# Retention in a two-block kernel: V projected token-major, value matmuls moved behind the next head's first unit, gate units reordered

## The reference

```python
def second_block(x, ...):
    h = rmsnorm(x, g_mix)
    proj = h @ w_in
    xc, gb, gc, q, k, v, g_sw, gate_a, gate_r = split(proj, ...)
    y_a = (gb * conv(gc * xc)) @ w_a_out
    qf = rotary(q by heads) * 256 ** -0.5        # 4 heads, 256 wide
    kf = rotary(k by heads)
    vf = v by heads                              # 4 heads, 512 wide
    ret = retention forward + strict retention backward (qf, kf, vf)
    # = ((q k^T) * decay(n - m)) v for each head, over all 512 x 512 pairs
    ret = (ret - mean) * rsqrt(var + EPS) * g_ret        # over the 512 of a head
    y_r = (ret * silu(g_sw)) @ w_r_out
    merged = sigmoid(gate_a) * y_a + sigmoid(gate_r) * y_r
    x = x + merged @ w_o
    x = x + ffn(rmsnorm(x))
    return rmsnorm(x)
```

## Time and profile before

| | |
|---|---|
| median of 3 runs | 1593.28 us (1589.33 to 1594.75) |
| span of the profiled execution, first to last instruction | 1585.1 us |
| TensorE busy in the span | 1515.8 us, 96% |
| VectorE, ScalarE, GpSimd busy | 704.2, 589.0, 92.0 us |
| mean granted clock of TensorE | 0.973 of full |
| the four heads of the retention stage | 665.38 to 923.09 us, 257.71 us |

### The profile page before, as it was taken

One profiled execution on the slowest core, in us unless ns is written; L12 is line 12 of the kernel. 1 busy time (PEld: TensorE's weight loads), 2 busy tenths in 40 slices (PEclk: granted clock), 3 DMA queues, 4 the chain that ended last, 5 costly groups with the idle time before them and its releaser, 6 DMA issues.

```text
span 1585.1 us, 20029 instructions
## 1 busy us (share of the span) xinstructions
PE 1515.8 (96%) x7068; PEld 1247.0 (79%) x7068; DVE 704.2 (44%) x1078; ACT 589.0 (37%) x955; POOL 92.0 (6%) x97
## 2 busy tenths in 40 slices
PE   7799998998989999999999999999998999999997
PEld 4578886887768888887787878887876888888886
DVE  4443256764465442344453524454445333333332
ACT  5232335653433334333333344443333333332321
POOL 5100500000000000000000023210000000000000
PEclk9799899998989999999999999999998999999999
DMA  9963320000333333331121213325232333333321
GB/s 328 328 135 95 106 60 9 1 2 14 89 134 89 100 97 102 93 94 53 53 80 52 79 54 93 93 80 157 82 96 63 106 93 93 105 92 99 99 84 53
DMA packets 243191, 147.87 MB, mean 93 GB/s; under 512 B 21490, under 2 KB 237758, under 8 KB 241732
## 3 DMA queue, kind: packets, MB, share of 16 engines
q1 hardware_dynamic: 239652, 131.63, 28.5%
q0 software_dynamic: 3488, 15.58, 2.9%
HBM read 138.81 MB, written 7.34 MB: 92 GB/s over the span
## 4 chain that ended last, share of the span: by engine, by line
PE 67%; issue 25%; DMA 3%; DVE 2%; ACT 2%; POOL 0%; DVEq 0%; POOLq 0%; SPq 0%; ACTq 0%
PE ps L368 50%; PE ps L1449 3%; PE ps L1731 3%; PE ps L1627 3%; PE ps L1641 2%; DMA w_raw<-in_w_in_dram 2%; PE ps L1708 1%; PE ps L1471 1%; PE ps L1526 1%; DMA bias_line<-bias_lines 1%; PE ps L1519 1%; DVE ret_val L1386 0%; PE ps L1615 0%; DMA rel_bias_sb<-in_rel_bias_dram 0%; PE ps L1494 0%
## 5 line engine op out<-in xcount | busy, mean ns | idle before, releaser
L385 DVE TENSOR_TENSOR w_lo<-w_raw,w_hi 128x1024 fp32r<-128x1024 f32 (+1 forms) x221 | 268.2, 1218 | 324.5 <-ACT w_hi L380 320.7
L380 ACT ACTIVATE w_hi<-w_raw 128x1024 fp32r<-128x1024 f32 (+1 forms) x221 | 228.9, 1043 | 32.4 <-DMA w_raw<-in_w_in_dram 18.8
L368 PE MATMUL ps<-g_hi,w_hi 128*128 128x512 f32 x704 | 181.0, 399 | 1.9 <-ACT g_hi L789 1.6
L368 PE MATMUL ps<-g_hi,w_lo 128*128 128x512 f32 x704 | 175.6, 392 | 0.0
L368 PE MATMUL ps<-g_lo,w_hi 128*128 128x512 f32 x704 | 174.1, 390 | 0.0
L368 PEld LDWEIGHTS ps<-g_hi,w_hi 128*128 128x128 f32 x704 | 131.8, 189 | 33.5 <-issue 4.9
L368 PEld LDWEIGHTS ps<-g_hi,w_lo 128*128 128x128 f32 x704 | 133.3, 189 | 28.1
L368 PEld LDWEIGHTS ps<-g_lo,w_hi 128*128 128x128 f32 x704 | 132.5, 188 | 27.6
L392 ACT ACTIVATE temps<-ps 128x512 f32<-128x512 f32 x68 | 40.7, 598 | 262.2 <-PE ps L368 262.2
L368 PE MATMUL ps<-f_hi,w_hi 128*128 128x512 f32 x352 | 90.3, 398 | 1.6 <-ACT f_hi L789 1.6
L368 PE MATMUL ps<-f_hi,w_lo 128*128 128x512 f32 x352 | 88.6, 395 | 0.0
(11 more groups left out here) (329 smaller groups left out, 2141.7 us busy)
## 6 DMA issues: line engine op xcount, KB each, us to landing
w_raw<-in_w_in_dram SPq DMA_DIRECT2D x95, 512.0 KB, 3.9
w_raw<-in_w_ff_gate_dram SPq DMA_DIRECT2D x22, 512.0 KB, 3.8
w_raw<-in_w_ff_up_dram SPq DMA_DIRECT2D x22, 512.0 KB, 3.7
w_raw<-in_w_in_dram SPq DMA_DIRECT2D x36, 256.0 KB, 4.3
w_ada_shift_scale<-in_w_ada_dram SPq DMA_DIRECT2D x8, 1024.0 KB, 20.2
w_raw<-in_w_r_out_dram SPq DMA_DIRECT2D x16, 512.0 KB, 4.3
w_raw<-in_w_ff_down_dram SPq DMA_DIRECT2D x16, 512.0 KB, 4.2
w_ada_gate<-in_w_ada_dram SPq DMA_DIRECT2D x2, 2048.0 KB, 12.9
```

The lines of the kernel that those rows point to most:

```text
L368: mm = pe.matmul(bank, w[:, slot, k], mov[:, k0 + k], start=first and n == 0 and k == 0, stop=last and n == 2 and k == kts - 1)
L380: act.activation(whi[:, slot, 0:kts], raw[:, slot, 0:kts], ACT.Copy).then_inc(hi_done, 1)
L385: nc.vector.tensor_tensor(wlo[:, slot, 0:kts], raw[:, slot, 0:kts], whi[:, slot, 0:kts].bitcast(F32), ALU.subtract).then_inc(lo_done, 1)
```

## The change

- V is projected token-major. Each of the four v units of a head now holds two of the eight 128-row blocks of the head's 1024 x 512 weights (`load_rows`: rows of 512 floats in place of 128), and the unit runs 4 x 6 matmuls with a block of the activations stationary and the 512 weight columns moving (`v_unit`). The four units add up in PSUM banks 4 to 7, one bank for each block of 128 tokens. The transposes and `v_t` are gone; `v_hi` and `v_lo` are made from the banks after the last v unit.
- The scores go before the fourth v unit, into banks 0 to 3. The p products are made at step 6 of the head, the v split at step 7.
- The value matmuls of a head (`read_out`) run after the first q unit of the next head; those of the last head after the first gate unit.
- POOL starts on a head's sum when that head's `ret` is there, no longer after all 16 tiles.
- The gate units of a head come as four silu, then two sigmoid.
- The two loops over heads are written out on every engine; `strip2` and the raw q have other places.

```diff
-PHASE_OUTS = (16, 8, 1, KT, 3 * KT, 2 * KT, 8 * RET_HEADS, 16 + KT, KT, KT, 2 * FT, KT)
+PHASE_OUTS = (16, 8, 1, KT, 3 * KT, 2 * KT, 4 * RET_HEADS, 16 + KT, KT, KT, 2 * FT, KT)
...
-RS_BANK = [4, 5, (O_QKV + 4) % 4, (O_QKV + 5) % 4]
-PV_BANK = [5, 6, 7, 4]
+RS_BANK = [(O_QKV + j) % 4 for j in range(4)]
...
-        strip2 = sb("strip2", [P, STRIP], R + 87)
-        v_t = sb("v_t", [P, 2, S], R + 91)
+        strip2 = sb("strip2", [P, STRIP], R + 107)
+        q_raw = sb("q_raw", [P, 2, S], R + 91)
...
-        qk_raw = sb("qk_raw", [P, 4, S], R + 131)
+        k_raw = sb("k_raw", [P, 2, S], R + 131)
...
+        def half_rows(t, u):
+            return t[:, u % SLOTS].rearrange("p k n -> p (k n)").rearrange("p (a n) -> p a n", a=2)
...
+            def load_rows(u, src):
+                sp.wait_ge(hi_done, u - 3)
+                sp.wait_ge(lo_done, u - 3)
+                sp.dma_start(half_rows(raw, u), src).then_inc(raw_in[u % SLOTS], 16)
...
-            with sp.Fori(0, 4) as it:
-                for k in range(8):
-                    if k < 4:
-                        cut = it * 256 + (3072 + 1024 * (k // 2) + (k % 2) * P)
-                    else:
-                        cut = it * 512 + (5120 + (k - 4) * P)
-                    load(it, 8, U_QKV + k, w_in2_v[:, :, wide(cut)])
...
+            for h in range(RET_HEADS):
+                for k in range(4):
+                    cut = h * 256 + 3072 + 1024 * (k // 2) + (k % 2) * P
+                    load(None, 0, U_QKV + 8 * h + k, w_in2_v[:, :, cut:cut + P])
+                for c2 in range(4):
+                    load_rows(U_QKV + 8 * h + 4 + c2, w_in2_v[:, 2 * c2:2 * c2 + 2, 5120 + 512 * h:5632 + 512 * h])
+            for h in range(RET_HEADS):
+                for n in range(6):
+                    cut = 7168 + h * 512 + n * P if n < 4 else GR_COL + h * 256 + (n - 4) * P
+                    load(None, 0, U_GATE + 6 * h + n, w_in2_v[:, :, cut:cut + P])
...
-            pool.wait_ge(m["ret_ev"], 16)
...
+            for h in range(RET_HEADS):
+                pool.wait_ge(m["ret_ev"], 4 * h + 4)
+                if h:
+                    pool.wait_ge(m["mu_mm"], h)
...
+            def ret_out(h):
+                for t in range(4):
+                    act.wait_ge(m["rpv_mm"], 4 * h + t + 1)
+                    a.activation(ret[:, 4 * h + t], ps[:, 4 + t], ACT.Copy).then_inc(m["ret_ev"], 1)
...
+            for h in range(RET_HEADS):
                 for k in range(8):
-                    act_convert(act, it, 8, U_QKV + k + AHEAD)
-                    dst = qk_raw[:, k] if k < 4 else v_t[:, k % 2]
-                    act_out(act, it, 8, U_QKV + k, dst, O_QKV + k, ACT.Copy)
+                    u = U_QKV + 8 * h + k
+                    act_convert(act, None, 0, u + AHEAD)
+                    if k == 0 and h == 0:
+                        act.wait_ge(lo_done, u + AHEAD + 1)
+                    if k < 4:
+                        act_out(act, None, 0, u, (q_raw if k < 2 else k_raw)[:, k % 2], O_QKV + 4 * h + k, ACT.Copy)
+                    if k == 0 and h:
+                        ret_out(h - 1)
...
-                    if k >= 5:
-                        v_round(k - 5)
-                for j in range(3):
-                    p_round(j)
-                v_round(3)
-                p_round(3)
-                for t in range(4):
-                    count = at(it, 4, t + 1)
-                    apart(act, it)
-                    act.wait_ge(m["rpv_mm"], count)
-                    a.activation(tile_of(ret, it, 4, t), ps[:, PV_BANK[t]], ACT.Copy).then_inc(m["ret_ev"], 1)
...
+                    if k == 6:
+                        for j in range(4):
+                            act.wait_ge(m["pm_done"], 4 * h + j + 1)
+                            a.activation(p_hi[:, j], p_f[:, j % 2], ACT.Copy).then_inc(m["ph_done"], 1)
+                    if k == 7:
+                        act.wait_ge(unit_done, u + 1)
+                        for j in range(NI):
+                            a.activation(v_hi[:, j], ps[:, 4 + j], ACT.Copy).then_inc(m["vh_done"], 1)
...
+            for h in range(RET_HEADS):
+                for n in range(6):
+                    u, o = U_GATE + 6 * h + n, O_GATE + 6 * h + n
+                    act_convert(act, None, 0, u + AHEAD)
+                    if n < 4:
+                        act_out(act, None, 0, u, sg[:, n], o, ACT.Silu)
                     else:
-                        act_out(act, it, 12, U_GATE + k, tile_of(sig_r, it, 4, 2 * hh + n), O_GATE + k, ACT.Sigmoid)
+                        act_out(act, None, 0, u, sig_r[:, 2 * h + n - 4], o, ACT.Sigmoid)
+                    if n == 0 and h == 0:
+                        ret_out(RET_HEADS - 1)
...
-                def v_rest(t):
-                    dve.wait_ge(m["vh_done"], at(it, 4, t + 1))
-                    cut = slice(t * P, (t + 1) * P)
-                    v.tensor_tensor(v_lo[:, :, cut], ps[:, 4 + t].rearrange("p (j e) -> p j e", j=NI),
-                                    v_hi[:, :, cut].bitcast(F32), ALU.subtract).then_inc(m["vl_done"], 1)
...
-                    if k in (5, 6):
-                        v_rest(k - 5)
-                dve.wait_ge(m["decay_done"], at(it, 1, 1))
-                p_mult(0)
-                p_mult(1)
-                p_rest(0)
-                v_rest(2)
-                p_mult(2)
-                p_rest(1)
-                v_rest(3)
-                p_mult(3)
-                p_rest(2)
-                p_rest(3)
-                own.end(RET_HEADS)
...
+                    if k == 6:
+                        dve.wait_ge(m["decay_done"], h + 1)
+                        p_mult(0)
+                        p_mult(1)
+                        p_rest(0)
+                        p_mult(2)
+                        p_rest(1)
+                        p_mult(3)
+                        p_rest(2)
+                        p_rest(3)
+                    if k == 7:
+                        for j in range(NI):
+                            dve.wait_ge(m["vh_done"], 4 * h + j + 1)
+                            v.tensor_tensor(v_lo[:, j], ps[:, 4 + j], v_hi[:, j].bitcast(F32),
+                                            ALU.subtract).then_inc(m["vl_done"], 1)
...
-            with pe.Fori(0, RET_HEADS) as it:
-                def v_trans(t):
-                    pe.wait_ge(evac, at(it, 8, O_QKV + 5 + t))
-                    for j in range(NI):
-                        mm = trans(ps[:, 4 + t, blk(j)], v_t[:, t % 2, blk(j)])
-                    mm.then_inc(m["vtr_mm"], 1)
-                def scores(j):
+            def v_unit(h, c2):
+                u = U_QKV + 8 * h + 4 + c2
+                pe.wait_ge(hi_done, u + 1)
+                pe.wait_ge(lo_done, u + 1)
+                if h and c2 == 0:
+                    pe.wait_ge(m["ret_ev"], 4 * h)
+                for j in range(NI):
+                    for n, (x, w) in enumerate(((g_hi, whi), (g_hi, wlo), (g_lo, whi))):
+                        for kk in range(2):
+                            mm = pe.matmul(ps[:, 4 + j], x[:, 2 * c2 + kk, blk(j)], half_rows(w, u)[:, kk],
+                                           start=c2 == 0 and n == 0 and kk == 0, stop=c2 == 3 and n == 2 and kk == 1)
+                mm.then_inc(unit_done, 1)
+            def scores(h):
+                pe.wait_ge(m["qkl_done"], 4 * h + 4)
+                for j in range(4):
                     for n, (k, q) in enumerate(((k_hi, q_hi), (k_lo, q_hi), (k_hi, q_lo))):
                         for t in range(2):
                             mm = pe.matmul(ps[:, RS_BANK[j]], k[:, t, blk(j)], q[:, t], start=n == 0 and t == 0,
                                            stop=n == 2 and t == 1)
                     mm.then_inc(m["rs_mm"], 1)
-                for k in range(8):
-                    pe_unit(pe, it, 8, U_QKV + k, 8, O_QKV + k, g_hi, g_lo)
-                    if k >= 5:
-                        v_trans(k - 5)
-                pe.wait_ge(m["qkl_done"], at(it, 4, 4))
-                for j in range(4):
-                    if j < 2:
-                        pe.wait_ge(m["vl_done"], at(it, 4, j + 1))
-                    scores(j)
-                v_trans(3)
-                pe.wait_ge(m["pm_done"], at(it, 4, 2))
+            def read_out(h):
                 for t in range(4):
-                    if t in (1, 2):
-                        pe.wait_ge(m["vl_done"], at(it, 4, t + 2))
                     for n, (w, p) in enumerate(((v_hi, p_hi), (v_lo, p_hi), (v_hi, p_lo))):
                         for j in range(NI):
-                            if t == 0 and n != 1:
-                                pe.wait_ge(m["ph_done" if n == 0 else "pl_done"], at(it, 4, j + 1))
-                            mm = pe.matmul(ps[:, PV_BANK[t]], w[:, j, blk(t)], p[:, j], start=n == 0 and j == 0,
+                            if t == 0:
+                                pe.wait_ge(m[("ph_done", "vl_done", "pl_done")[n]], 4 * h + j + 1)
```

(77 more changed lines are left out.)

106 lines of the change are left out of this document (35 added, 71 removed).

## The result

| | before | changed |
|---|---|---|
| median of 4 executions each | 1591.3 us (1587.63 to 1594.75) | 1566.05 us (1565.14 to 1568.15) |
| ratio, 95% interval | | 0.9847 [0.9825, 0.9869] |
| span of the profiled execution | 1585.1 us | 1564.4 us |

The kernel became 1.5% faster. Three later groups of 15 to 23 executions put the kernel before at 1588.8, 1588.6 and 1588.7 us, and the changed one, run again twice, at 1567.2 and 1566.5. The gain is about 22 us, not 25 and not 18.

What follows compares the result with a forecast made beforehand. TensorE, busy 96% of the span, was taken to bound the kernel; 7.3 us of transposes, 9.5 of stall and 1.6 of the clock's fall gave 18.3 us off 1593.28, so 1575.0 us, range 1569 to 1580.

Steps and rivals of the forecast that it cites:

- transposes: Retention heads: the 16 transposes of v a head go, saving 1.83 us a head, 7.3 us in four.
- stall: Value matmuls: TensorE's 2.23 us wait for p's rounding and 0.14 behind it go each head, 9.5 us in four.
- the sum: Four retention heads: 239.4 us against 257.71, a gain of 18.3 us from transposes, stall and the clock's fall.
- the loops: Loops over heads written out: no gap at the loop's turn in TensorE's trace, so 0.
- the clock's fall: Third retention head, behind its stall: granted clock falls, 1.6 us, expected not to happen once the stall is gone.
- the v unit at 5.44 us and full clock: Retention heads: 24 matmuls a v unit, as many as before, 5.44 us; upper end 5.57, worth 2.1 us.
- the rival of the lower clock: V units changing bank every 6 matmuls run at the lower clock, 4.8 us more each; 0.04, shared with other outweighing losses.
- No new wait in the heads: Retention heads: p chain and v split end hidden behind other units, so TensorE gets no new stall; 0.80.
- the cover: Next head's first q unit, 5.44 us, hides the v split of about 3.6 us, leaving 1.9 us.
- The gate stage's wait: Before the first mean matmul: 0.98 us wait for POOL's sum goes, 1.0 us for the `ret` copy comes; net 0.
- Gate units reordered: Gate stage: same six units, ACT swaps tables as often beside TensorE, so nothing; 2.4 us if that cover failed.
- From the span to the median: Whole kernel: the same 18.3 us taken from span 1585.1 to 1566.8 and from median 1593.28 to 1575.0.

Runs made afterwards that it cites:

- the last experiment: Loops written out and each head's stall filled with 8 idle matmuls, against the kernel before: 1583.19 us median against 1588.67, ratio 0.996.

## Why the prediction was wrong in its range and right in its mechanism

The two large terms, transposes and stall, came out to 0.1 us (16.8 us forecast, 16.7 left in the last experiment). The forecast of 1575.0 us is 8.8 us above the 1566.2 that the measured terms give, and two steps made that. The start: the sum was taken from 1593.28 us where the kernel before has 1588.7, 4.6 us. And two small terms: the loops, put at 0, 2.4 us, and the clock's fall, put at 1.6, 3.3 us. From the right start the sum of 18.3 us would still have given 1570.4. Point by point:

- *Transposes*: forecast 1.83 us a head, measured 1.88 by putting them back. Right.
- *The stall*: forecast 2.23 us and 0.14 behind it. With both, a head goes from 64.03 to 59.84 us, where I had 59.85. Right, and so is the v unit at 5.44 us and full clock; the rival of the lower clock didn't come. Of the oscillation that the Trainium skill (TensorE: Matmul & The Clock Gate, section A second HAM failure mode: psum-queue depth-cycling) tells of, this kernel shows nothing at 6 matmuls a bank.
- *No new wait in the heads*: right; the cover is 2.1 us where I had 1.9.
- *The gate stage's wait*: 1.0 us forecast for the `ret` copy, 0.84 measured. Right.
- *Gate units reordered*: no time, as forecast. "ACT swaps its two function tables as often" holds for the gate stage, eight loads at the copies in either kernel, and fails behind it: 22 more loads in the feed-forward loop, all of them hidden.
- *Loops written out*: "So 0" was mis-sized. Alone they gave 2.4 us, not set apart from zero by themselves; on top of the filled stalls 2.3. I had looked for a gap at the turn of the retention loop on TensorE alone; the cost lay behind it, in the gate loop, on ScalarE, which reloads its table at the turn, and on GpSimd, which starts later. From the profiles: 0.5 us of a shorter wait for the first sum, 0.6 in the gate stage, 0.2 to 0.3 at the start of YR. Where the other 1.1 us of the median come from stays open.
- *The clock's fall*: I counted one, 1.6 us, since the profile showed one. Filling the stalls gave 3.3 us: two on average.
- *From the span to the median*: the step that failed. I wrote "From the span 1585.1 to 1566.8, and from the median 1593.28 to 1575.0", which takes the 8.2 us between the two as a constant. An execution takes 1.8 us more than its span. That puts the profiled one at about 1586.9 us, among the shortest, and the three timed ones held two of the upper group near 1594. That three executions gave 1593.28 was bad luck; to take the gap as a constant was the mistake. Over 58 executions the kernel before has a median near 1588.7. My range used the bounds of the falls in the heads only, and started them from 1593.28, so its low end couldn't reach 1566.

The sum with the measured terms: 1588.7 - 16.8 (transposes and stall, 4 x 4.19) - 3.3 (falls) - 2.4 (loops) = 1566.2 us, against 1566.05 to 1567.18 measured. The small terms carry intervals of some 2 us either way, so the agreement to 0.2 us is in part luck. The experiment with both small terms checks it from the other side.

On the profiled pair: 1585.1 to 1564.4 is 20.7 us. From the start of the heads to the first mean it is 264.14 - 245.64 = 18.5 (forecast 18.3); behind it 2.5: gate stage 0.6, YR 0.3, the norm 1.5, the end 0.1; the changed kernel reached the heads 0.3 us later. The norm's 1.5 us can't be put down to the change, as the second repetition of the changed kernel has 13.9 us there.

**What stays open.** The upper group, about 6 us up. Counted as more than 5 us above the fastest of its kernel, 27 of 104 executions with the old order of the retention stage lay in it, and 1 of 32 with the new order (1570.16 us). The place seen for it, in one profile, is ahead of anything that the change touches, and I have no mechanism by which the change would reach back. The variant with both small terms, old order, had none in 10 either. It doesn't enter the medians of the larger groups much, but it made the first comparison look like 25 us.

## What to carry to other kernels

When a forecast is carried from a profile to timed runs, first ask where the profiled execution lies among them: the gap between its span and the median is a constant only if the runs say so. A short stall on TensorE can cost more than its length when the clock falls behind it, and one profile shows only whether it fell that time; filling the stall with idle matmuls prices it. A loop's turn has to be looked for on every engine, not only on the one that bounds the kernel. And a stretch whose length differs between two profiles is a cost of the change only if repeated profiles of one kernel agree on it: the second norm took 12.6 and 13.9 us in the same program.

## What the runs showed of the hardware

- Idle matmuls made the kernel faster: 32 of them, 7.3 us of TensorE time placed in 8.9 us of stalls, took 3.3 us off the median (interval 0.2 to 4.8); the granted clock of the profiled heads was 1.00.
- A stall isn't enough for a fall: 2.0 us idle behind transposes and three matmuls was followed by one in 5 of 12 profiled heads (three profiles), 1.5 us idle behind full units in none of four.
- The same 64 matmuls of 64 columns took 7.14 us at granted clock 1.00 in one execution and 11.19 us at 0.62 in another of the same kernel. With the unit behind them the fall cost 6.45 us.
- ScalarE reloads its function table at the turn of a hardware loop: ten loads of 1.28 us at one line became four when the loops were written out.
- What stands ahead of a hardware loop decides on the loads in it: with silu the last function ahead of the feed-forward loop it had no table load, with sigmoid the last it had two of 1.28 us at each of 11 turns. Under a busy TensorE they cost no time (653.1 us in both).
